# The down-projection of a gated MLP as seven half-size products instead of eight, in a fused float32 decoder layer

## The reference

```python
def conv_ffn(h, w_up, conv_w, conv_b, w_down):
    u = h @ w_up                                   # (1024 x 1024) @ (1024 x 4096)
    u = lax.conv_general_dilated(u, conv_w[:, None, :], window_strides=(1,),
                                 padding=[(2, 0)], feature_group_count=c) + conv_b   # width 3, causal
    gate, val = jnp.split(u, 2, axis=-1)
    return (jax.nn.gelu(gate) * val) @ w_down      # (1024 x 2048) @ (2048 x 1024)
...
x = x + conv_ffn(rms_norm(x, norm_ffn[i]), w_up[i], conv_w[i], conv_b[i], w_down[i])
```

## Time and profile before

| what | us |
|---|---|
| median of three runs | 1445.81 |
| the profiled execution | 1446.5 |
| its span, first to last instruction | 1444.7 |
| TensorE busy in it | 1383.6 (96%) |
| VectorE busy in it | 713.5 (49%) |
| GpSimd busy in it | 455.6 (32%) |
| ScalarE busy in it | 372.4 (26%) |
| mean granted TensorE clock | 0.991 of full speed |

### The profile page before, as it was taken

The page is one execution under the profiler, slowest core; times in us unless marked ns, Lnnn a source line. Parts: engine busy times, 40 slices in busy tenths (PEclk is TensorE's granted clock), DMA queues, the critical chain, the costliest instruction groups (busy, mean ns, idle before and its releaser), DMA issues.

```text
span 1444.7 us, 18559 instructions
## 1 busy us (share of the span) xinstructions
PE 1383.6 (96%) x7421; PEld 1105.8 (77%) x7421; DVE 713.5 (49%) x1187; ACT 372.4 (26%) x727; POOL 455.6 (32%) x230
## 2 busy tenths in 40 slices
PE   5999889999999899999899999999999999999998
PEld 4888557799777656666688888788888888888887
DVE  5796676535454766656554410623223223365641
ACT  5322554400211344444311200521111111132110
POOL 4213002234723111101143444244344334345442
PEclk9999999999999999999999999999999999999999
DMA  7420101032111000000011141421211211141122
GB/s 186 47 54 19 45 1 30 18 76 56 37 37 37 19 19 19 1 19 20 19 37 51 44 160 44 147 59 44 58 44 44 58 44 44 58 160 44 53 76 90
DMA packets 126823, 76.46 MB, mean 53 GB/s; under 512 B 39312, under 2 KB 113424, under 8 KB 126736
## 3 DMA queue, kind: packets, MB, share of 16 engines
q1 hardware_dynamic: 126752, 75.46, 18.8%
HBM read 66.93 MB, written 8.52 MB: 52 GB/s over the span
## 4 chain that ended last, share of the span: by engine, by line
PE 88%; DVE 7%; ACT 3%; issue 2%; DMA 0%; SPq 0%; ACTq 0%; DVEq 0%
PE ps L675 24%; PE ps L677 24%; PE ps L676 24%; PE ps L1155 3%; PE ps L1188 2%; PE ps L1172 2%; PE ps L913 1%; PE ps L930 1%; PE ps L943 1%; PE ps L690 1%; DVE merged L1827 1%; DVE small L2019 1%; ACT arena L1299 1%; PE ps L887 1%; DVE arena L1579 1%
## 5 line engine op out<-in xcount | busy, mean ns | idle before, releaser
L586 POOL TENSOR_TENSOR wh<-raw,zero 128x1024 fp32r<-128x1024 f32 (+2 forms) x85 | 172.3, 2027 | 863.9 <-PE ps L677 848.6
L675 PE MATMUL ps<-hTh,wh 128*128 128x512 f32 x1008 | 402.3, 399 | 2.7 <-ACT arena L1389 1.9
L677 PE MATMUL ps<-hTh,wl 128*128 128x512 f32 x1008 | 393.9, 391 | 0.0
L676 PE MATMUL ps<-hTl,wh 128*128 128x512 f32 x1008 | 393.4, 390 | 0.0
L589 POOL TENSOR_TENSOR wl<-raw,wh 128x1024 fp32r<-128x1024 f32 (+2 forms) x93 | 257.3, 2767 | 100.1 <-ACT wh L1335 93.4
L675 PEld LDWEIGHTS ps<-hTh,wh 128*128 128x128 f32 x1008 | 190.0, 188 | 46.8 <-issue 7.3
L677 PEld LDWEIGHTS ps<-hTh,wl 128*128 128x128 f32 x1008 | 189.6, 188 | 40.3
L676 PEld LDWEIGHTS ps<-hTl,wh 128*128 128x128 f32 x1008 | 190.1, 189 | 37.5 <-issue 0.5
L677 PE MATMUL ps<-wh,hTl 128*128 128x512 f32 (+2 forms) x512 | 179.1, 350 | 0.0
L676 PE MATMUL ps<-wl,hTh 128*128 128x512 f32 (+2 forms) x512 | 179.0, 350 | 0.0
L675 PE MATMUL ps<-wh,hTh 128*128 128x512 f32 (+2 forms) x512 | 179.0, 350 | 0.0
(11 more groups left out here) (331 smaller groups left out, 1652.8 us busy)
## 6 DMA issues: line engine op xcount, KB each, us to landing
raw<-in_w_in SPq DMA_DIRECT2D x35, 512.0 KB, 3.9
raw<-in_w_up SPq DMA_DIRECT2D x32, 512.0 KB, 4.0
raw<-in_w_down SPq DMA_DIRECT2D x16, 512.0 KB, 3.7
merged<-in_x SPq DMA_DIRECT2D x8, 512.0 KB, 7.4
raw<-in_w_out SPq DMA_DIRECT2D x8, 512.0 KB, 3.5
merged<-in_x SPq DMA_DIRECT2D x2, 2048.0 KB, 10.2
x_keep<-merged SPq DMA_DIRECT2D x2, 2048.0 KB, 11.0
conv<-x_keep SPq DMA_DIRECT2D x1, 2048.0 KB, 9.4
```

Source lines behind the costliest of these rows:

```text
L586: eng.tensor_tensor(wh[:, p, 0:n], raw[:, p, 0:n], zero1[:, 0:1].broadcast_to((P, n)), ALU.add).then_inc(s_hi[0], 1)
L675: mm(out_, ah, bh, start=first, stop=False, skip_group_check=True)
L676: mm(out_, ah, bl, start=False, stop=False, skip_group_check=True)
L677: return mm(out_, al, bh, start=False, stop=last, skip_group_check=True)
```

## The change

Everything up to the down-projection stays, apart from added work that runs beside the up-projection. The down-projection becomes Winograd's form of Strassen's algorithm: `act` and `w_down` are cut into 2x2 blocks (512 tokens by 1024 channels, and 1024 channels by 512 columns), and seven products of blocks take the place of eight. Each product has eight pieces `c` of 128 channels, four token blocks a piece, and an `mm3` for each, so 12 matmuls a piece. Two pieces make a pair `f`; there are 28 pairs.

- The four combinations of `w_down` blocks that the algorithm needs are made beside the up-projection: SP loads four times four blocks of 512 KB to `vsum`, GpSimd makes 16 additions of 128x1024 (`sum_v`), and SP stores the results to `v_dram`.
- The loops over `j` on SP and GpSimd are written out.
- In the down-projection ScalarE rounds the weights (128x512 a piece, `dn_weight_high`, 56 of them), and GpSimd makes only the subtraction (128x512 a piece). Weight buffers become five slots of 512 columns.
- ScalarE rounds 28 activation pairs of 128x2x512 (`dn_high`), VectorE subtracts them (`dn_low`).
- VectorE makes 12 combinations of `act` blocks in the buffer of low parts (`dn_sum`) and 8 in place (`dn_s3`, `dn_d`).
- VectorE adds 28 banks to the residual (`y_out`); some outputs get two contributions. A product uses four banks, and consecutive products use alternate sets.
- The residual is loaded in four DMAs of 1 MB, and the output is stored in six DMAs.

```diff
+        DN_LEFT = ["a11", "a12", "n2", "s1", "s3", "s4", "a22"]
+        DN_RIGHT = [("w", 0, 0), ("w", 1, 0), ("v", 1), ("v", 0), ("v", 2), ("w", 1, 1), ("v", 3)]
+        DN_SUM = {2: 0, 3: 4, 5: 8}
+        def dn_consumed(eng, c):
+            if c % 8 == 7:
+                eng.wait_ge(S("y_ready"), 4 * (c // 8 + 1))
             else:
+                eng.wait_ge(S("dn_used"), c + 1 - c // 8)
         @block.sync
+            for j in range(1, 16):
                 for k in range(2):
+                    eng.wait_ge(S("fw_split"), 2 * j + (k - 1))
                     load_up(j, k)
+                if 2 <= j < 14 and j % 3 == 2:
+                    load_v(j // 3)
+                if 2 <= j < 14 and j % 3 == 1:
+                    save_v(j // 3 - 1)
+            for f in range(NPAIR):
...
+                    eng.wait_ge(S("fw_split"), 32 + 2 * (f - 1))
...
+                if f == 4:
                     eng.wait_ge(S("act_done"), 16)
+                    eng.wait_ge(S("dn_used"), 4)
                     eng.wait_ge(S("x2_saved"), 32)
+                if f in (4, 6, 8, 10):
+                    load_res({4: 0, 6: 2, 8: 3, 10: 1}[f])
         @block.gpsimd
+                    split(k ^ SWAP, 1024, S(f"fw_in{k}"), 16 * j + 16, (S("fw_hi"), 2 * j + (k + 1)), S("fw_split"))
+                    if 2 <= j < 13 and j % 3 != 1:
+                        sum_v(j // 3 - (j % 3 == 0), 2 * (j % 3 == 0) + k)
+            for c in range(NPIECE):
+                eng.wait_ge(S("fw_hi"), 33 + c)
+                eng.tensor_tensor(wlf[:, dn_slot(c)], dn_raw(c), whf[:, dn_slot(c)].bitcast(F32), ALU.subtract
+                                  ).then_inc(S("fw_split"), 1)
         @block.tensor
+            for c in range(NPIECE):
+                m, kc, f = c // 8, c % 8, c // 2
+                ah, al = dn_split(f)
+                eng.wait_ge(S("fw_split"), 33 + c)
+                if c % 2 == 0:
+                    eng.wait_ge(S("dn_x"), f + 1)
+                for tb in range(4):
+                    if kc == 0:
+                        if m < 2:
+                            eng.wait_ge(S("up_read"), 29 + 2 * m + tb // 2)
                         else:
+                            eng.wait_ge(S("y_added"), 4 * (m - 2) + tb + 1)
+                    t = slice(tb * P, (tb + 1) * P)
+                    ins = mm3(ps[:, 4 * (m % 2) + tb, :], ah[:, c % 2, t], al[:, c % 2, t],
+                              whf[:, dn_slot(c)], wlf[:, dn_slot(c)], m in (0, 1, 3) and kc == 0, kc == 7)
         @block.scalar
+            def dn_high(f):
+                m, u = f // 4, f % 4
...
+                elif f >= 8:
+                    dn_consumed(eng, 2 * (f - 8) + 1)
+                if m in DN_SUM:
+                    eng.wait_ge(S("dn_sum"), DN_SUM[m] + u + 1)
+                elif m == 4:
+                    eng.wait_ge(S("dn_in_place"), u + 1)
...
+            def dn_weight_high(c):
+                if c < 5:
+                    eng.wait_ge(S("up_done"), 31 + (c > 2))
                 else:
+                    dn_consumed(eng, c - 5)
...
+            for f in range(4, 8):
+                dn_high(f)
+                dn_weight_high(f + 1)
+            for c in range(9, NPIECE):
+                dn_weight_high(c)
+                f = (c + 5) // 2
+                if c % 2 and 8 <= f < NPAIR:
+                    dn_high(f)
         @block.vector
+            def y_out(m):
+                g, hf = [(0, 0), (0, 0), (1, 0), (1, 1), (1, 1), (1, 0), (0, 1)][m]
...
+                    tt(a, a, ps[:, 4 * (m % 2) + tb, :], ALU.subtract if g else ALU.add).then_inc(S("y_added"), 1)
...
+            dn_low(2)
+            dn_low(3)
+            dn_s3(0)
+            dn_low(4)
+            dn_sum(8)
+            dn_low(5)
+            dn_s3(1)
+            dn_sum(9)
+            dn_low(6)
+            dn_low(7)
+            dn_s3(2)
+            dn_sum(10)
+            dn_low(8)
+            dn_s3(3)
+            dn_sum(11)
+            for f in range(9, NPAIR):
+                if f % 4 == 3:
+                    y_out((f - 11) // 4)
+                if 12 <= f + 1 < NPAIR:
+                    dn_sum(f + 1)
+                dn_low(f)
+                if 16 <= f + 1 < 20:
+                    dn_d(f - 15)
+            y_out(5)
+            y_out(6)
```

More of the change, by code:

```diff
@@ L96, in program @@
         hTh = sb("hTh", [P, KC, L], F32R)
+        plain = ExitStack()
+        low32 = sb("low32", [P, KC, L], at=plain)
+        plain.close()
         hTl = sb("hTl", [P, KC, L], F32R)
@@ L146, in program @@
         ffn.close()
+        vflat = res1[:, :, :].rearrange("p a b -> p (a b)")
+        vsum = [vflat[:, 1024 * i:1024 * (i + 1)] for i in range(4)]
         res = [conv[:, :, :, :].rearrange("p a b (c n) -> p (a b c) n", n=HALF), res1[:, :, :]]
@@ L557, in _ @@
+            for t0, t1 in ((4, 6), (6, 7), (7, 8)):
+                eng.wait_ge(S("y_added"), 20 + t1)
+                eng.dma_start(out[0, t0 * P:t1 * P, 0:HALF].rearrange("(t p) d -> p t d", p=P),
+                              res[0][:, t0:t1, :]).then_inc(S("stored"), 16)
+            eng.wait_ge(S("stored"), 96)
         @block.gpsimd
@@ L2123, in _, with dn_sum @@
             eng.wait_ge(S("x2_saved"), 32)
[L2124 to L2127, removed]
+            def dn_sum(f):
+                m, u = f // 4, f % 4
+                if m not in DN_SUM:
+                    return
+                a11, a12, a21, a22 = [act_part(k, hf, u) for hf in range(2) for k in range(2)]
+                whole = dn_plain(f)
+                dn_consumed(eng, 2 * (f - 8) + 1)
+                if m == 2:
+                    eng.wait_ge(S("dn_in_place"), u + 1)
+                    ins = stt(whole, a11, -1.0, a22, ALU.mult, ALU.subtract)
+                elif m == 3:
+                    ins = tt(whole, a22, a21, ALU.subtract)
+                else:
+                    eng.wait_ge(S("dn_in_place"), u + 5)
+                    ins = tt(whole, a11, a12, ALU.add)
+                ins.then_inc(S("dn_sum"), 1)
@@ new lines, in dn_low, with dn_s3, dn_d @@
+            def dn_low(f):
+                high, low = dn_split(f)
+                eng.wait_ge(S("dn_hi_x"), f + 1)
+                src = dn_plain(f) if f // 4 in DN_SUM else dn_direct(f)
+                tt(low, src, high.bitcast(F32), ALU.subtract).then_inc(S("dn_x"), 1)
+            def dn_s3(u):
+                a11, a12, a21, a22 = [act_part(k, hf, u) for hf in range(2) for k in range(2)]
+                tt(a11, a11, a21, ALU.subtract).then_inc(S("dn_in_place"), 1)
+            def dn_d(u):
+                a11, a12, a21, a22 = [act_part(k, hf, u) for hf in range(2) for k in range(2)]
+                tt(a12, a22, a12, ALU.subtract).then_inc(S("dn_in_place"), 1)
@@ L2131, in _ @@
                     ffn_pair(jj, u)
-            for cg in range(2):
-                act_low(cg)
+            for f in range(2):
+                dn_low(f)
             for u in range(2):
                 ffn_pair(7, u)
[L2137 to L2149, removed]
+            eng.wait_ge(S("act_done"), 16)
+            dn_low(2)
[18 more added lines that the diff above has]
+                    dn_sum(f + 1)
+                dn_low(f)
+                if 16 <= f + 1 < 20:
+                    dn_d(f - 15)
+            y_out(5)
+            y_out(6)
 _INS = ['x', 'norm_mix', 'w_in', 'nsa_q_gain', 'nsa_k_gain', 'cmp_pe', 'cmp_wk', 'cmp_wv',
```

179 lines of the change are left out of this document (107 added, 72 removed).

## The result

The changed kernel takes 1423.76 us (median of four runs, 1422.92 to 1425.08), the kernel before 1447.01 beside it. The way and nearly the whole size are right; the one stand of TensorE that the sum counted did not happen. Two later sets of runs of the same kernel gave 1424.28 and 1424.38, against 1448.13 and 1446.65 for the kernel before.

What follows compares the result with a forecast made beforehand. TensorE, busy 96% of the span, was taken to bound the kernel. Terms: -21.8 for matmuls, +1.0 for a stand, 0 for the end, so -20.8: median 1445.8 to 1425.0 us, range 1423.8 to 1431.

Steps and rivals of the forecast that it cites:

- The matmuls gone: Down-projection: 768 matmuls become 672, 96 fewer at 0.2268 us each, 21.8 us less.
- Beside the up-projection at 0: Up-projection: GpSimd's 16 additions and SP's loads and stores of block sums are hidden, costed at 0.
- Turns: Last stage: VectorE two-SBUF-input instructions and GpSimd pieces alternate, each whole, at 1.1 and 1.1 to 1.2 us.
- the upper bound: First deadline with VectorE at 1.22 and GpSimd at 1.63 us: 53.8, said to be 11.7 us late.
- the first rival: Last stage: turns cost 2.85 us a pair, TensorE waits at pieces 16 and 32, 4 to 11 us; chance 0.20.
- Adds from PSUM outside the turns: Last stage: VectorE's `y_out` adds, with one PSUM input, cost 0.69 us and take no turns with GpSimd.
- The first deadline: Before product 2, `y_out(0)` must make its first add by t = 43.5 us; forecast done at 44.2.
- the stand of 1.0: Before product 2, TensorE stands 0.7 us, with small hand-overs of the next three banks 1.0.
- lower bound: First deadline: a stand of 0, if not all 17 GpSimd subtractions get in front of the first adds.
- a shorter end: After the last matmul: final add and store costed at 0, with -0.3 to +0.6 us.
- the second rival: Last stage: TensorE waits before every 12 matmuls, 40 more waits at 0.1 us, 4 us, giving 1429; chance 0.06.
- the third rival: Last stage: raw weight loads set the pace, slower than before once landing takes 7.4 us; chance 0.04.

Runs made afterwards that it cites:

- as_is: The changed kernel timed again with no edit, beside the kernel before: 1424.28 us, ratio 0.9838.

## Why the prediction was right or wrong

*The matmuls gone: right.* 96 of them, 21.76 us in the profile against 21.8, and eight products through the new queues bring back the 173.96 us of before. This one term is the result.

*Beside the up-projection at 0: right*, shown by the run without that work, whose last stage begins 0.04 us earlier.

*Turns: right in kind and price.* VectorE's two-input instructions stretch from 1.21 to about 2.3 and a GpSimd piece stands in between. A pair cost 2.24 where the upper bound and the first rival had 2.85. 18 VectorE instructions of 1.13 and 15 GpSimd turns of 1.1 give 4.1 + 20.3 + 16.5 = 40.9, and 40.95 was measured. These two prices were fitted after the result (the prediction's own 1.1 and 1.15 give 41.2), but they hold elsewhere. With the VectorE instructions and the GpSimd turns that stood in front of the adds in each profile, 18 and 16 give 42.0 (the changed kernel's second profile, measured 42.2), 19 and 16 give 43.2 (adds one instruction later, measured 43.2), 20 and 17 give 45.4 (two later, 45.4), and 22 and 17 give 47.7 (differences early, 47.7).

*Adds from PSUM outside the turns: right.* They took 0.67 to 0.69 in all 28 cases. The Trainium skill ("SBUF — State Buffer", Who interferes with whom) states that a VectorE instruction with at most one SBUF input does not contend with GpSimd. The trace agrees, by the 0.67 to 0.69.

*The first deadline: wrong, and this is the step that failed:* "GpSimd subtracts pieces 3 to 19 meanwhile, 17". The three profiles of the changed kernel have 15, 16 and 15 in front of the adds. Piece 19 is never there in time, piece 18 in one of them. Their slots come free when TensorE has used pieces 13 and 14, at t = 38.1 and 40.8, and the rounding on ScalarE comes behind that. At the first of these times VectorE has two instructions left behind the one it is in, at the second it ends the last. Piece 18 can stand longer behind `dn_high(11)`, which waits for VectorE's `dn_sum(11)`: in the changed kernel's profile it began at t = 40.5. One or two turns of about 1.1 fewer put the adds that much earlier, and the stand of 1.0 (0.7 and the hand-overs) becomes a margin of 0.6 or 1.9. The prediction had this outcome as its lower bound ("not all 17 get in front") and did not follow when the slots come free, which would have decided it. That such a margin is all there is, the late adds show: one instruction more costs 0.5 us, two cost 4.2.

*The sum.* With the stand at 0 it reads -21.8, and the forecast would have been 1424.0. The three medians are 1423.76, 1424.28 and 1424.38. The low end of the range held no stand and a shorter end, and nothing for what a median of a few runs moves, 0.6 us here. By the prediction's own terms, 1.0 and 0.3 under 1425.0, it is 1423.7 and not 1423.8. So which side of the low end the median fell on is chance; that the stand of 1.0 did not happen is not. It is also luck that 1425.0 is so close: it rests on the kernel before at 1445.81, a median of three runs near its lowest, and with a fourth run that median is 1447.01, from which the same sum gives 1426.2.

*Two slips that changed nothing.* The upper bound of the first deadline puts the adds at 53.8 where 42.8 was needed; that is 11.0 late, not 11.7. The last add trails the end of its matmul by 0.03 in the rows (1440.48 + 0.39, then 1440.90), not 0.1. With that the second rival would have been smaller still.

*The medians differ by 22 to 24, the stages by 21.8.* The rest is not in the changed stage. The lowest runs of sets made together are 22.7, 22.2 and 21.9 apart. The median of the kernel before lies 1.4, 3.1 and 2.0 us above its lowest run, that of the changed kernel 0.8, 1.5 and 1.6. Much of this scatter is the granted clock: the lowest and the highest of the 17 runs of the kernel before that were made beside `as_is` had spans of 1443.3 at 0.989 and 1455.4 at 0.981, which is 15.9 and 27.7 us of clock not granted: 11.8 of the 12.1 between them. Why the kernel before had more of it in that set is not settled.

*The rivals.* Turns falling behind did not happen, but the kernel is near it: it is what four instructions in the wrong place, or rounding on GpSimd, bring about. A wait at every piece costs nothing: the stage with a wait before each 12 matmuls takes 0.2267 a matmul like the one before. The raw loads landed in 3.4 to 4.7 us, so the third rival's 7.4 was far. They did hold ScalarE up for 10 us in all, at most 4.2 at once, all inside the lead.

## What to carry to other kernels

Where TensorE is busy without a gap, matmuls taken away count in full, and the question is only whether the rest still fits. Fit is not a matter of busy shares (GpSimd 130 of 152 us would have passed). It is counted up to each deadline: which instructions stand in front of it on the engine, and how many of the other engine's turns can come in between, given when *those* are released. Keep two-input SBUF work that feeds a later product behind the adds that free PSUM, and put rounding on the engine that takes no turns: ScalarE's 56 of the weights, 128x512 each, took 0.61 to 0.64 us, all of them.

## What the runs showed of the hardware

A stand of TensorE can cost more than itself. After 2.4 us and after 4.7 us idle in a stage that was otherwise full, the granted clock was 0.50, the 1.2 GHz level, for over 3 us; in the first case 9 matmuls took 1.6 us longer, in the second the stage grew by 1.7 more than the 4.9 by which the start came late. In the second case the clock fell only when TensorE was at work again: it started at 1318.55, and the stretches around that are

```profile
1318.50:1319.20 0.70, 0.66 (x3) 0.99 0.00 0
1319.20:1322.60 3.40, 3.40 (x10) 0.50 0.03 5
```

After 0.2 us idle it stayed at 1.00. It also stayed at 1.00 over the stretches of the run with rounding on GpSimd, where TensorE stood 1.2 us in front of many pieces.

VectorE instructions with two SBUF inputs and GpSimd's took strict turns as long as both had work: 2.24 us for a pair of a 128x1024 on VectorE and a 128x512 subtraction on GpSimd, which take 1.21 and 1.29 alone.
